# The weight splits behind three norms on VectorE, a third panel rounded before the second root, and the first two down panels interleaved by rows, in a two-layer decoder step

## The chip, the cores and the metric

The kernel runs on one core of one Trainium2 chip. A core has TensorE (matrix products into PSUM), VectorE, ScalarE, GpSimd (POOL in the profile), and SyncE, whose queue starts the loads. The metric is the device time of one execution in microseconds (us): lower is better.

## The reference

One inference step of a decoder with an S5 layer followed by a FoX attention layer, over 512 prompt tokens and 8 sample tokens. The width is 1024, so each activation is held as eight tiles of 128 channels by 520 tokens. What matters here is what stands around the norms and in the feed-forward part of both layers:

```python
x = x + rmsnorm(o, p['norm_mix_post'][l])
f, cp = conv_ffn(rmsnorm(x, p['norm_ffn_pre'][l]), p['w_up'][l], p['conv_w'][l],
                 p['conv_b'][l], p['w_down'][l], conv_prev[l])
x = x + rmsnorm(f, p['norm_ffn_post'][l])
...
def conv_ffn(h, w_up, cw, cb, w_down, prev):
    u = h @ w_up
    y, new_prev = causal_dwconv(u, prev, cw, cb)
    g, val = jnp.split(y, 2, axis=-1)
    return (jax.nn.silu(g) * val) @ w_down, new_prev
```

All of it is in float32, w_up is 1024 by 5632 and w_down is 2816 by 1024.

## The kernel before

**Products in three parts.** A float32 weight panel of 128 output channels is loaded into `raw[slot]` by SyncE, rounded by ScalarE into `w_hi[slot]` (`hi`, line 2062), and its rest `raw - w_hi` is written to `w_lo[slot]` by GpSimd (`lo`, line 919; a *split* below). TensorE adds w_hi·x_hi, w_hi·x_lo and w_lo·x_hi in PSUM (`product`, line 2546). There are two slots, taken in turn, so panel q+2 can be rounded only when panel q has been multiplied (`panel_done`), can be split only behind its rounding, and its PSUM banks must have been read (`panel_read`). Panels are numbered through the whole program. `PH[name]` holds a phase's rows per panel, panel count and first number.

**The phases.** `wout0`, `up00`, `down00`, `up01`, `down01` are the output projection and the feed-forward part of layer 0; `win1` is the input projection of layer 1; `wout1`, `up10`, `down10`, `up11`, `down11` follow for layer 1. The feed-forward width is done in two halves: an up phase has 22 panels of 8 rows of 128, in 11 pairs (gate and value), and a down phase 8 panels of 11 rows. A down panel's row k needs the k-th product of gate and value, `h_hi` and `h_lo`.

**Inside an up phase.** For each pair VectorE scales the PSUM result by `rstd` into `uc` (lines 1747 and 1748, which frees the banks), waits for ScalarE's first tap `yc` (line 2405), adds the two other taps (lines 1752 to 1758), does the same for the second panel, then multiplies by ScalarE's `sg = silu(...)` (line 2411) and writes `h_hi` and `h_lo` (lines 1763 to 1767). ScalarE's program for a pair is: round the even panel, `newconv`, `yc`, round the odd panel, `newconv`, `yc`, `silu`. [...] The pairs are a hardware loop (`act.Fori` in `run`); the compiler puts the loads of ScalarE's function tables (ACT_TABLE_LOAD) where a function needs another set, and at the head of a loop it must suit both the entry and the way back.

**At a norm.** `post_norm` on VectorE and `post` on ScalarE walk through 16 steps (two token halves by eight channel tiles): scale y, add to x, split x into `x_hi` (ScalarE) and `x_lo` (VectorE), and sum squares on TensorE for the next norm. TensorE starts on the first two panels behind the norm meanwhile (`first_pair`, line 2643). The constants `ROOT_1`, `HI_NEXT`, `ROOT_PRE` and `RECIP_PRE` say at which step ScalarE takes the root of the second half's statistics, rounds the second next panel, and takes the next norm's first root, and at which step VectorE inverts it. Before, GpSimd splits both panels and ScalarE rounds the third one (the first that TensorE multiplies behind `first_pair`) in the first turn of the phase's loop, behind the last root.

## Time and profile before

| | |
|---|---|
| time, median of 3 runs | 1584.65 us (1578.77 to 1586.68) |
| profiled execution | 1581.49 us, its span 1579.8 us, mean granted clock 0.951 |
| TensorE busy | 1431.8 us, 91% of the span |
| VectorE busy | 986.8 us, 62% |
| ScalarE busy | 625.3 us, 40% |
| GpSimd busy | 671.0 us, 42% |

Times in rows are microseconds from the span's start. In a row of the timeline the first number is the start, the second the length; a bracket gives how long the engine had been idle and who released it. A busy share is an average over all phases: what a change is worth in one phase is read there.

### The profile page before, as it was taken

Reading aid. Unit: us, or ns where it says so; the run is one execution under the profiler, and the core shown is the slowest. Engines: PE = TensorE matmul, PEld = TensorE weight load, DVE = VectorE, ACT = ScalarE, POOL = GpSimd, SP = SyncE. Lnnn points to the kernel's source line nnn. Section 1 sums busy time; section 2 is a strip of 40 time slices with the busy share of each in tenths; the row PEclk is TensorE's granted clock in tenths of the full one; section 3 lists DMA queues with packets and bytes.
Section 4 is the critical chain, followed back from the end, with each engine's and each line's share of the span. In section 5 each row is a group of like instructions: output and inputs, shape, how many; then the busy total and the mean of one; then the engine's idle time right before and its main releaser. Section 6 shows DMA issues by size and latency. Waiting matters only on the chain.

```text
span 1579.8 us, 32525 instructions
## 1 busy us (share of the span) xinstructions
PE 1431.8 (91%) x12097; PEld 1325.2 (84%) x12097; DVE 986.8 (62%) x1644; ACT 625.3 (40%) x1058; POOL 671.0 (42%) x429
## 2 busy tenths in 40 slices
PE   6987848988998999999898979998979999999997
PEld 6975637978998999999798966555969999999997
DVE  5769945577775056765847678642587772277755
ACT  4554533245663134332414225431356551234323
POOL 0686232313333444443277888401323443344440
PEclk9996978989999999999999999988989999999999
DMA  5444372222333223333044758995213233223321
GB/s 169 125 96 77 67 199 66 76 55 68 95 82 95 79 83 93 91 96 92 27 132 140 229 162 286 320 319 154 80 38 88 88 108 92 78 83 92 113 79 60
DMA packets 288905, 180.46 MB, mean 114 GB/s; under 512 B 54072, under 2 KB 274396, under 8 KB 288748
## 3 DMA queue, kind: packets, MB, share of 16 engines
q1 hardware_dynamic: 288812, 179.20, 39.3%
q8 instruction: 61, 1.00, 0.3%
q14 instruction: 32, 0.26, 0.1%
HBM read 167.10 MB, written 10.63 MB: 113 GB/s over the span
## 4 chain that ended last, share of the span: by engine, by line
PE 58%; issue 15%; DVE 12%; POOL 6%; ACT 3%; SPq 3%; DMA 2%; DVEq 1%; ACTq 0%; POOLq 0%
PE big L2546 48%; PE big L2612 3%; SPq L583 2%; PE misc L2697 2%; ACT yc L2405 1%; DVE y L1663 1%; POOL s5s L923 1%; POOL e_tmp L923 1%; DVE tmp L1202 1%; POOL e_r L923 1%; POOL e_i L923 1%; PE big L2643 1%; DVE rstd L1160 1%; DVE hf L1763 1%; DVE x_lo L1192 1%
## 5 line engine op out<-in xcount | busy, mean ns | idle before, releaser
L919 POOL TENSOR_TENSOR w_lo<-raw,w_hi 128x1024 fp32r<-128x1024 f32 (+2 forms) x163 | 427.3, 2622 | 741.1 <-ACT w_hi L2062 740.9
L2546 PE MATMUL big<-x_hi,w_hi 128*128 128x264 f32 x2008 | 414.8, 288 | 17.2 <-POOL w_lo L919 12.4
L2062 ACT ACTIVATE w_hi<-raw 128x1024 fp32r<-128x1024 f32 (+2 forms) x179 | 198.4, 1109 | 533.8 <-PE big L2546 494.3
L2546 PE MATMUL big<-x_hi,w_lo 128*128 128x264 f32 x2008 | 407.6, 285 | 0.0
L2546 PE MATMUL big<-x_lo,w_hi 128*128 128x264 f32 x2008 | 405.9, 284 | 0.0
L2546 PEld LDWEIGHTS big<-x_hi,w_hi 128*128 128x128 f32 x2008 | 312.0, 190 | 23.2 <-issue 16.3
L2546 PEld LDWEIGHTS big<-x_lo,w_hi 128*128 128x128 f32 x2008 | 311.8, 190 | 0.0
L2546 PEld LDWEIGHTS big<-x_hi,w_lo 128*128 128x128 f32 x2008 | 310.9, 190 | 0.0
L1752 DVE SCALAR_TENSOR_TENSOR yc<-uc,convw,yc 128x512 f32<-128x512 f32 x88 | 120.2, 1366 | 113.3 <-ACT yc L2405 113.3
L2546 PE MATMUL big<-h_hi,w_hi 128*128 128x264 f32 x616 | 126.1, 286 | 10.6 <-DVE h_lo L1767 9.2
L2546 PE MATMUL big<-h_lo,w_hi 128*128 128x264 f32 x616 | 124.9, 284 | 0.0
L2546 PE MATMUL big<-h_hi,w_lo 128*128 128x264 f32 x616 | 124.4, 283 | 0.0
L2546 PEld LDWEIGHTS big<-h_hi,w_hi 128*128 128x128 f32 x616 | 95.0, 190 | 11.8 <-DVE h_lo L1767 10.0
L2546 PEld LDWEIGHTS big<-h_hi,w_lo 128*128 128x128 f32 x616 | 95.3, 190 | 0.0
L2546 PEld LDWEIGHTS big<-h_lo,w_hi 128*128 128x128 f32 x616 | 95.2, 190 | 0.0
L1757 DVE SCALAR_TENSOR_TENSOR yc<-uc,convw,yc 128x512 f32<-128x512 f32 x88 | 84.7, 962 | 12.7 <-DVE yc L1755 0.2
L1056 POOL TENSOR_TENSOR areas<-areas,qb 128x768 f32<-128x768 f32 x41 | 75.1, 1847 | 11.8 <-DMA areas<-in_cache_k 10.8
L1780 DVE COPY y<-big 128x264 f32 (+1 forms) x32 | 12.2, 424 | 104.3 <-PE big L2546 104.3
L2405 ACT ACTIVATE yc<-uc,convw 128x520 f32<-128x520 f32 x88 | 72.3, 822 | 0.8
L1142 DVE TENSOR_TENSOR sumsq<-sumsq,sq 128x520 f32<-128x520 f32 x20 | 53.0, 2649 | 11.6 <-ACT sq L2361 9.9
L2401 ACT ACTIVATE newconv<-uc 128x10 f32 (+1 forms) x88 | 18.1, 205 | 103.9 <-DVE uc L1748 103.8
L2643 PE MATMUL big<-x_hi,w_hi 128*128 128x264 f32 (+1 forms) x96 | 38.2, 398 | 17.0 <-DVE x_lo L1192 16.6
(425 smaller groups left out, 2385.6 us busy)
## 6 DMA issues: line engine op xcount, KB each, us to landing
raw<-in_w_up SPq DMA_DIRECT2D x88, 512.0 KB, 3.9
raw<-in_w_down SPq DMA_DIRECT2D x32, 704.0 KB, 4.7
areas<-in_cache_v SPq DMA_DIRECT2D x42, 384.0 KB, 4.5
areas<-in_cache_k SPq DMA_DIRECT2D x41, 384.0 KB, 4.3
raw<-in_w_in SPq DMA_DIRECT2D x16, 512.0 KB, 4.2
raw<-in_w_out SPq DMA_DIRECT2D x16, 512.0 KB, 4.3
raw<-in_w_kv SPq DMA_DIRECT2D x12, 512.0 KB, 4.1
spare<-in_cache_k SPq DMA_DIRECT2D x12, 384.0 KB, 4.1
```

The costliest lines, as they stand in the source:

```text
L583: sp.dma_start(dst, src, **kw).then_inc(s_(sm), 16)
L919: pool.tensor_tensor(w_lo[slot][:, 0:kb, :], raw[slot][:, 0:kb, :], w_hi[slot][:, 0:kb, :].bitcast(F32), ALU.subtract).then_inc(lo_made, 1)
L923: own.do(pool.tensor_tensor(o, a_, b_, op))
L1056: own.tell(pool.tensor_tensor(p, p, qb[b % 2][:].rearrange("p (a d) -> p a d", a=2), ALU.mult), s_("k_product"), n + 1)
L1142: ins = V.tensor_tensor(sumsq[:], sumsq[:], sq[:, m % 2, :], ALU.add)
L1752: st(V.scalar_tensor_tensor(yy[:, 0:T], uu[:, 1:1 + T], w_[1], yy[:, 0:T], ALU.mult, ALU.add))
L1757: st(V.scalar_tensor_tensor(yy[:, 0:T], uu[:, 0:T], w_[0], yy[:, 0:T], ALU.mult, ALU.add))
L2062: A.activation(w_hi[slot][:, 0:kb, :], raw[slot][:, 0:kb, :], ACT.Copy).then_inc(hi_made, 1)
L2405: A.activation(yy[:], uu[:, 2:2 + NT], ACT.Identity, bias=convw[:, 1 - l, bass.ds(it + (f * KH + half * KF + 132), 1)], scale=convw[:, 1 - ...
L2546: ins = pe.matmul(big[2 * slot + b_][:, 0:c1 - c0], w[slot][:, k, :], r[:, c0:c1], start=(k == 0 and n_ == 0), stop=(k == kb - 1 and n_ == 2))
L2612: return pe.matmul(big[2 * slot + b_][:, 0:c1 - c0], w[slot][:, k, :], r[:, c0:c1], start=(k == 0 and n_ == 0), stop=(k == kb - 1 and n_ = ...
L2643: ins = pe.matmul(big[2 * slot + b_][:, 0:c1 - c0], w[slot][:, k, :], r[:, k, c0:c1], start=(k == 0 and n_ == 0), stop=(k == KD - 1 and n_ ...
```

## The change

Three things are changed. At the three norms that are followed by a projection (`wout0`, `down01`, `wout1`) VectorE splits the first two panels behind the norm, at steps 1 and 11 of `post_norm`, and GpSimd no longer does; `ROOT_1` goes from 4 to 6 and `HI_NEXT` from 5 to 8. ScalarE rounds the third panel before the last root, so `run` gets an argument `rounded=3` for `up00`, `up10` and `win1`: the first turn of its loop is then written out ahead of the loop, less that rounding. And in `down00` and `down10` TensorE multiplies rows 0 to 9 of both first panels, then row 10 of each, in `pair_by_rows`.

```diff
-ROOT_1, HI_NEXT, ROOT_PRE, RECIP_PRE = 4, 5, 10, 13
+ROOT_1, HI_NEXT, ROOT_PRE, RECIP_PRE = 6, 8, 10, 13
+LO_FIRST, LO_NEXT = 1, 11
...
                 if name == "win1":
-                    lo(base, base % 2, kb)
-                    lo(base + 1, (base + 1) % 2, kb)
                     for i in range(2, n):
...
                 first = 2 if name in ("glu", "up00", "up10") or n <= 2 else 0
-                for i in range(min(first, n) if name != "glu" else 0):
+                for i in range(n if n <= 2 else 0):
                     lo(base + i, (base + i) % 2, kb)
...
                         split_lo(k, x[:, k, c], gain(nxt, k, nl), c)
+                    if nxt is not None and i == LO_FIRST:
+                        lo(PH[ph][2] + 8)
+                    elif nxt is not None and i == LO_NEXT:
+                        lo(PH[ph][2] + 9)
...
-            def run(name, work=None, ahead=True, started=True):
+            def run(name, work=None, ahead=True, started=True, rounded=2):
...
                 pairs = n // 2
+                if rounded > 2:
+                    work(0, 0)
+                    hi(kb, base + 3)
+                    work(0, 1)
                 if pairs > 2:
-                    with act.Fori(0, pairs - 1) as it:
+                    with act.Fori(rounded - 2, pairs - 1) as it:
...
                         root_half(name, 0)
+                hi(KD, base + n + 2)
                 root_half(name, 1)
...
-                    run(f"up{l}{f}", work)
+                    run(f"up{l}{f}", work, rounded=2 if f else 3)
...
-                if isinstance(it, int) and half == 0:
+                if isinstance(it, int) and it and half == 0:
...
-            run("win1", first_queries)
+            run("win1", first_queries, rounded=3)
...
+            def pair_by_rows(base, rhs, wait_k):
+
+                for rows_ in (range(KH - 1), (KH - 1,)):
+                    for q in (base, base + 1):
+                        if rows_[0] == 0:
+                            pe.wait_ge(lo_made, q + 1)
+                            pe.wait_ge(panel_read, q - 1)
+                        for k in rows_:
+                            wait_k(k)
+                            xh, xl = rhs(k)
+                            for n_, (w, r) in enumerate(((w_hi, xh), (w_hi, xl), (w_lo, xh))):
+                                for b_, (c0, c1) in enumerate(HALF):
+                                    ins = pe.matmul(big[2 * (q % 2) + b_][:, 0:c1 - c0], w[q % 2][:, k, :], r[:, c0:c1],
+                                                    start=(k == 0 and n_ == 0), stop=(k == KH - 1 and n_ == 2))
+                        if rows_[0]:
+                            ins.then_inc(panel_done, 1)
...
                     if f == 0:
-                        phase(f"down{l}{f}", h_half, wait_k=h_made)
+                        pair_by_rows(PH[f"down{l}0"][2], h_half, h_made)
+                        phase(f"down{l}0", h_half, first=2)
                         continue
```

ScalarE's instructions of `up00` before, from the last root of the norm through the loop body (registers and branches left out). `sd` is the root, `w_hi` a rounding, `sg` the silu:

```order
L2091 ACTIVATE sd<-misc,eps 128x256
...
L2062 ACT_TABLE_LOAD
L2062 ACTIVATE w_hi<-raw 128x1024
...
L2405 ACTIVATE yc_122<-uc_120,convw 128x520
...
L2062 ACTIVATE w_hi<-raw 128x1024
...
L2405 ACTIVATE yc_123<-uc_121,convw 128x520
...
L2411 ACT_TABLE_LOAD
L2411 ACTIVATE sg<-yc_122 128x520
L2073 REGISTER_ALU
L2073 COMPARE_AND_BRANCH
```

The same place with the change: the first rounding stands ahead of the root, the rest of the first pair ahead of the loop, and the loop begins at the second rounding below.

```order
L2065 ACTIVATE w_hi<-raw 128x1024
L2098 ACTIVATE sd<-misc,eps 128x256
...
L2419 ACT_TABLE_LOAD
L2419 ACTIVATE sg<-yc_122 128x520
...
L2065 ACTIVATE w_hi<-raw 128x1024
...
L2413 ACTIVATE yc_122<-uc_120,convw 128x520
...
L2065 ACTIVATE w_hi<-raw 128x1024
...
L2413 ACTIVATE yc_123<-uc_121,convw 128x520
L2418 REGISTER_ALU
L2419 ACTIVATE sg<-yc_122 128x520
L2080 REGISTER_ALU
L2080 COMPARE_AND_BRANCH
```

Two table loads stood in the loop of `up00`; the written-out first pair now holds one, and the loop none. The same holds for `up10`.

TensorE at the first pair of `down00` before, around row 10 of the first panel (`big0` and `big1` are its banks, `big2` and `big3` the second panel's):

```order
L2546 MATMUL big0<-h_hi_118,w_lo0 128x264
L2546 MATMUL big1<-h_hi_118,w_lo0 128x256
L2546 MATMUL big0<-h_hi_118,w_hi0 128x264
L2546 MATMUL big1<-h_hi_118,w_hi0 128x256
L2546 MATMUL big0<-h_lo_119,w_hi0 128x264
L2546 MATMUL big1<-h_lo_119,w_hi0 128x256
```

And with the change, the last twelve matmuls of the two panels and what stands ahead of them:

```order
L2649 MATMUL big2<-h_hi_118,w_lo1 128x264
L2649 MATMUL big3<-h_hi_118,w_lo1 128x256
L2649 MATMUL big0<-h_hi_118,w_hi0 128x264
L2649 MATMUL big1<-h_hi_118,w_hi0 128x256
...
L2649 MATMUL big0<-h_hi_118,w_lo0 128x264
L2649 MATMUL big1<-h_hi_118,w_lo0 128x256
L2649 MATMUL big2<-h_hi_118,w_hi1 128x264
L2649 MATMUL big3<-h_hi_118,w_hi1 128x256
```

Row 10 of the first panel, the one that ends it, has moved behind rows 0 to 9 of the second, so both panels end within twelve matmuls.

## Rows read from the trace of the kernel before

**Rows 1.** Page, part 1: busy us, share of the span, instructions

```profile
PE 1431.8 (91%) x12097; PEld 1325.2 (84%) x12097; DVE 986.8 (62%) x1644; ACT 625.3 (40%) x1058; POOL 671.0 (42%) x429
```

**Rows 2.** Timeline of `up00`, one pair, engine by engine

```profile
470.68 1.28 ACT L2411 ACT_TABLE_LOAD   x1
...
472.63 1.28 ACT L2062 ACT_TABLE_LOAD   x1
473.93 1.06 ACT L2062 ACTIVATE w_hi<-raw 128x1024 fp32r<-128x1024 f32 x1
...
465.78 2.39 POOL L919 TENSOR_TENSOR w_lo<-raw,w_hi 128x1024 fp32r<-128x1024 f32 x1 [0.78 <-ACT w_hi L2062]
475.07 2.38 POOL L919 TENSOR_TENSOR w_lo<-raw,w_hi 128x1024 fp32r<-128x1024 f32 x1 [6.89 <-ACT w_hi L2062]
...
464.49 1.07 DVE L1752 SCALAR_TENSOR_TENSOR yc<-uc,convw,yc 128x512 f32<-128x512 f32 x1 [1.33 <-ACT yc L2405]
...
465.84 2.88 DVE L1757 SCALAR_TENSOR_TENSOR yc<-uc,convw,yc 128x512 f32<-128x512 f32 x1
...
471.85 0.75 DVE L1757 SCALAR_TENSOR_TENSOR yc<-uc,convw,yc 128x512 f32<-128x512 f32 x1
...
474.86 0.43 DVE L1747 TENSOR_TENSOR uc<-big,rstd 128x264 f32<-128x264 f32 x1
...
477.58 0.51 PE L2546 MATMUL big<-x_hi,w_hi 128*128 128x264 f32 x2 [0.65 <-POOL w_lo L919]
```

**Rows 3.** Timeline of `up00`, last turn (no table reload), and the `h_lo` before

```profile
486.29 3.22 POOL L919 TENSOR_TENSOR w_lo<-raw,w_hi 128x1408 fp32r<-128x1408 f32 x1 [5.80 <-ACT w_hi L2062]
...
474.24 0.70 DVE L1767 TENSOR_TENSOR h_lo<-hf,h_hi 128x520 f32 x1
...
486.56 3.52 DVE L1767 TENSOR_TENSOR h_lo<-hf,h_hi 128x520 f32 x1
490.00 0.42 DVE L1747 TENSOR_TENSOR uc<-big,rstd 128x264 f32<-128x264 f32 x1
```

**Rows 4.** Timeline, VectorE: first `uc` of `up00`; first, third, last pair of `up10`

```profile
363.24 0.43 DVE L1747 TENSOR_TENSOR uc<-big,rstd 128x264 f32<-128x264 f32 x1 [0.24 <-DVE uc L1726]
...
1179.30 0.43 DVE L1747 TENSOR_TENSOR uc<-big,rstd 128x264 f32<-128x264 f32 x1 [0.23 <-DVE uc L1726]
...
1202.82 0.43 DVE L1747 TENSOR_TENSOR uc<-big,rstd 128x264 f32<-128x264 f32 x1
...
1295.09 0.43 DVE L1747 TENSOR_TENSOR uc<-big,rstd 128x264 f32<-128x264 f32 x1
```

**Rows 5.** Windows, first pair of `up00` and `up10`: busy times, clock, DMA

```profile
363.00:375.70 12.70, 9.69 (x80) 9.70 (x81) 9.16 (x16) 7.52 (x10) 4.79 (x2) 1.00 0.31 86
1179.30:1191.80 12.50, 9.74 (x68) 9.74 (x69) 9.22 (x16) 7.35 (x10) 4.78 (x2) 0.86 0.29 86
```

**Rows 6.** Timeline of `up01`, whose loop holds no table load

```profile
578.43 1.06 ACT L2062 ACTIVATE w_hi<-raw 128x1024 fp32r<-128x1024 f32 x1 [3.34 <-PE big L2546]
```

**Rows 7.** Timeline of the first two panels of `down00` and of `down10`

```profile
502.70 0.80 PE L2546 MATMUL big<-h_hi,w_hi 128*128 128x264 f32 x2 [4.43 <-DVE h_lo L1767]
...
1307.95 0.51 PE L2546 MATMUL big<-h_hi,w_hi 128*128 128x264 f32 x2 [1.57 <-DVE h_lo L1767]
...
513.83 1.38 ACT L2062 ACTIVATE w_hi<-raw 128x1408 fp32r<-128x1408 f32 x1 [8.05 <-PE big L2546]
...
1316.86 1.38 ACT L2062 ACTIVATE w_hi<-raw 128x1408 fp32r<-128x1408 f32 x1 [6.50 <-PE big L2546]
```

**Rows 8.** Timeline of the norm between `wout0` and `up00`

```profile
329.97 3.10 DVE L1663 SCALAR_TENSOR_TENSOR y<-y,gains,rstd 128x264 f32<-128x264 f32 x2
...
341.79 0.49 DVE L1192 SCALAR_TENSOR_TENSOR x_lo<-x,gains,x_hi 128x264 fp32r<-128x264 f32 x1 [1.40 <-ACT x_hi L2103]
...
366.01 0.50 PE L2546 MATMUL big<-x_hi,w_hi 128*128 128x264 f32 x2 [3.37 <-POOL w_lo L919]
```

**Rows 9.** Tile `w_lo`, VectorE's splits in `win0`: ns min/median/max

```profile
L1149 DVE TENSOR_TENSOR w_lo<-raw,w_hi x16: 1207/1226/1705, 18.9 to 109.6; 128x1024 fp32r<-128x1024 f32 x16
```

## The prediction

> **What bounds the kernel now.** I read the busy shares first, then the waits of each phase that the change touches, then the timeline of single pairs of panels. TensorE is busy for 91% of the span and VectorE for 62% [rows 1], which looks like a kernel bound by its matmuls. The phases differ, though. Take the 10 pairs of `up10` that the rows span: from its third pair to its last, eight pairs take 1295.09 - 1202.82 = 92.27 us, 11.53 us each [rows 4]. There TensorE never waits; that is its own work. In `up00` nine pairs take 474.86 - 363.24 = 111.62 us, 12.40 us each [rows 2, 4], and TensorE stands 0.65 us for a split in the pair shown [rows 2]. What sets the 12.40 us is VectorE: it goes from one pair to the next with no wait but the ones for ScalarE's first tap `yc`, and its instructions stretch when GpSimd is in a split. Line 1757 takes 2.88 us around the split that starts at 465.78 [rows 2]; unhindered it takes 0.75 us (at 471.85), so 2.13 us are stall. Line 1752, at 1.07 us, loses another 0.32 us. The other split of the pair (475.07 to 477.45) falls mostly on the 1.3 us in which VectorE waits for `yc` anyway, and that is why it costs only those 0.32 us.
>
> So an up phase has two gaits. If TensorE is behind, ScalarE's roundings wait for it (3.34 us in `up01` [rows 6]), the splits fall where VectorE has time, and a pair takes 11.53 us. If VectorE is behind, roundings start as soon as ScalarE's program comes to them, and where the splits then fall decides the pair. The Trainium skill (SBUF — State Buffer, "SBUF: two separate sides") says that a VectorE operation with two SBUF inputs and a GpSimd operation take a shared port pair as an exclusive lock, and the loser blocks; by that rule, the trace agrees.
>
> **Part 1: the loads that vanish from the loop.** The order of ScalarE's instructions shows an effect that the edit does not name. With the first pair written out, the silu table is already loaded when the loop is entered, so both ACT_TABLE_LOADs leave the loops of `up00` and `up10`. They are 1.28 us each [rows 2]. ScalarE's order per pair is yc, load, silu, load, rounding. Without them the rounding at 473.93 starts 2.56 us earlier, at 471.4, and its split runs from about 472.5 to 474.9 instead of 475.07 to 477.45. TensorE does not hold it back: its panel has ended by then. But from line 1757 at 471.85 to the end of `h_lo` at 474.9 [rows 2, 3] VectorE works without a wait on operations that mostly read two SBUF tiles, and one of them has to stand out the split.
>
> What that costs can be read from the one turn that had no reload before: the last turn of `up00` [rows 3]. Its rounding follows the silu directly, the split runs from 486.29 for 3.22 us, and `h_lo` takes 3.52 us where it took 0.70 us a pair earlier: 2.82 us lost, 0.40 less than the split. That pair took 490.00 - 474.86 = 15.14 us. For a split of 2.38 us I take 2.38 - 0.40 = 2.0 us. The stall of line 1757 stays, since the odd rounding still follows yc at once. A pair then takes 12.40 - 0.32 + 2.0 = 14.1 us. TensorE, with 11.53 us of work, would stand 2.5 us in each.
>
> Does it get out of this gait? `up10` before did. Its first pair began like `up00`'s, but the clock was 0.86 there against 1.00 [rows 5], which held TensorE back by 12.5 x 0.14 = 1.75 us. At 12.40 us a pair TensorE has only 0.87 us to spare in each, so that was enough, ScalarE's odd rounding had to wait for TensorE, and from the third pair on the pair took 11.53 us. At 14.1 us TensorE has 2.6 us to spare in each pair, and one such dip is absorbed. So I expect the slow gait to hold through both phases.
>
> `up00`: nine pairs from 12.40 to 14.1, +15.3 us; the last pair keeps its 15.14 us. `up10`: ten pairs took 1295.09 - 1179.30 = 115.8 us [rows 4]; they will take 9 x 14.1 + 15.1 = 142.0 us, **+26.2 us**.
>
> Here a rule speaks against this. The Trainium skill (ScalarE: Activation LUTs, "What ACT_TABLE_LOAD costs") has a table switch at about 1.28 us for the load and 1.38 us more for a drain, and its advice is to have fewer of them. By that page alone 20 pairs with two loads less would be a gain; the sum above would have no +15.3 and no +26.2. The trace shows loads of 1.28 us with the next instruction right behind them. That ScalarE is relieved is true; it was not what VectorE waited for.
>
> **Part 2: down panels by rows.** Before, TensorE stands 4.43 us for the last `h_lo` in `down00` and 1.57 us in `down10` [rows 7]. Now it fills that time with rows 0 to 9 of the second panel. What is late next: both panels end together, and the third can be rounded only when the first has ended. Ten rows of six matmuls at 0.12 us are 7.2 us. In `down00` rows 0 to 9 of the first panel ended at 502.70 - 4.43 = 498.27; the second's would end at 505.5, the last rows at 506.2 and 506.9. Rounding 1.38 us [rows 7], split 3.22 us [rows 3] and hand-overs of 0.1 us bring the third panel to 510.9, a new wait of 4.0 us. Before it started when the second panel ended, at 513.8 [rows 7]. That is -2.9 us, measured from the last `uc` (490.00) 20.9 us instead of 23.8. In `down10` the same 20.9 us stand against 1316.86 - 1295.09 = 21.8 us [rows 4, 7]: -0.9 us. If `up10` were bound by TensorE, the new wait would cost more than it fills: 1306.38 + 7.2 + 0.7 + 4.7 = 1319.0 against 1316.9, +2.1 us.
>
> **Part 3: the norms.** GpSimd's split of the first panel stretched two of VectorE's scalings to 3.10 us, where an operation of that kind and shape takes 0.49 us: some 2.2 us lost [rows 8]. VectorE's own split takes 1.23 us [rows 9]. That is -1.0 us. The second split hinders one scaling for as long as they overlap, between 0 and 2 us, against another 1.23 us: I take nothing. With `ROOT_1` at 6 VectorE's wait of 1.40 us for `x_hi` [rows 8] goes, but the reciprocal two steps later needs that root: I take half, -0.7 us. The third rounding ahead of the root delays the root, the reciprocal and the first `uc` by up to 0.5 us: +0.4 us. Each norm gives -1.3 us. Bounds: +0.5 us if TensorE has to wait for the late split at step 11, -3.4 us if all of TensorE's wait behind the norm [rows 8] goes. The wait for the third panel's split does go, but behind it stands VectorE's `uc`, which frees the banks. Three norms: **-3.9 us**. `win1` gains only this.
>
> **The sum**, against the profiled execution's own 1581.5 us: +15.3 + 26.2 - 2.9 - 0.9 - 3.9 = +33.8, **1615 us**. The median of the runs shown is 3.2 us above that execution, and the three differ by 8 us; I say 1616. A measurement here tells about 0.5% (8 us) from no change.
>
> **The rivals.**
> - *Fast gait in both phases (1568 us).* Fewer table loads leave ScalarE free, TensorE binds `up00` and `up10` as it binds `up01`, whose loop has no load either [rows 6]. For it: `up01`. Against it: `up01` begins with TensorE behind VectorE, whereas behind a norm two panels are finished before the first `uc`, and VectorE would have to make good some 3 us while it loses 4. Price: from first `uc` to third down panel `up00` takes 513.8 - 363.2 = 150.6 us and `up10` 137.6; `up00` would fall to the latter, -13.0, by-rows costs 2.1 twice, norms -3.9: -12.7, and about 1 us more from `up10`'s first pairs. It decides if TensorE is held back by over 2.6 us in one pair. 0.16.
> - *One phase only (1592 us).* A dip of the clock tips one of the two: -3.9 + 15.3 - 2.9 + 2.1 = +10.6, or -3.9 - 13.0 + 2.1 + 26.2 - 0.9 = +10.5. 0.09.
> - *No effect in the loops (1576 us).* The even split costs VectorE no more than before: -3.9 - 2.9 + 2.1 = -4.7. Against it: the turn of rows 3. 0.07.
> - The forecast, slow gait in both: 0.68, with its own range 1603 to 1626 (2.2 us instead of 2.0 per split adds 4 us; norms at their bounds give -6 and +5; if the odd split's stall shrinks by 0.3 us, -6).
>
> **How the numbers follow.** Slower by over 0.5% (above 1592.6) holds the forecast and half of the one-phase case: 0.73. Faster (below 1576.7) holds the fast gait and a little of the no-effect case: 0.18. The rest is 0.09. The range that leaves out the fast gait and the ends of the forecast's is 1576 to 1626.
>
> **What the profile would show.** ACT_TABLE_LOAD once in each of `up00` and `up10`. From one `uc` of an even panel to the next, 14.1 us; two instructions among lines 1752 to 1767 of about 2.2 us more than usual in each pair; TensorE idle 2.5 us before even panels. In `down00` and `down10` no wait for `h_lo`, but some 4 us for the third panel's split. TensorE back behind the norms about 1.3 us earlier. Pairs of 11.5 us in `up00` would prove me wrong, and then the step that failed is that VectorE cannot catch up.

## The result, and the profile after

The changed kernel takes **1620.8 us** (median of 4 runs, 1617.9 to 1624.5) against 1581.7 us of the kernel before (4 runs, 1578.1 to 1586.7). The ratio is 1.0249, 95% interval 1.0218 to 1.0279: slower by 2.5%. The profiled execution took 1617.9 us, its span is 1616.2 us, 36.4 us longer than before (1579.8).

Page of the changed kernel, part 1 (it answers to [rows 1]):

```profile
PE 1448.9 (90%) x12097; PEld 1340.6 (83%) x12097; DVE 1027.1 (64%) x1650; ACT 571.8 (35%) x1020; POOL 655.7 (41%) x423
```

ScalarE lost 53.5 us of work, GpSimd 15.3 us. VectorE has six instructions more, and is busy 40.3 us longer: six splits of 1.22 us are 7.3 of them. The rest is no work, but instructions that got longer.

Timeline of the changed kernel, the second pair of `up00`: ScalarE, GpSimd, VectorE, TensorE (start, duration, engine, line, operation; in brackets the idle time before it and who ended it). It answers to [rows 2].

```profile
375.18 0.82 ACT L2413 ACTIVATE yc<-uc,convw 128x520 f32<-128x520 f32 x1
375.91 1.04 ACT L2065 ACTIVATE w_hi<-raw 128x1024 fp32r<-128x1024 f32 x1
...
381.82 0.62 ACT L2419 ACTIVATE sg<-yc 128x520 f32<-128x520 f32 x1
382.35 1.04 ACT L2065 ACTIVATE w_hi<-raw 128x1024 fp32r<-128x1024 f32 x1
...
377.03 2.40 POOL L920 TENSOR_TENSOR w_lo<-raw,w_hi 128x1024 fp32r<-128x1024 f32 x1 [4.01 <-ACT w_hi L2065]
383.47 2.64 POOL L920 TENSOR_TENSOR w_lo<-raw,w_hi 128x1024 fp32r<-128x1024 f32 x1 [4.05 <-ACT w_hi L2065]
...
374.04 0.43 DVE L1750 TENSOR_TENSOR uc<-big,rstd 128x264 f32<-128x264 f32 x1
...
377.18 2.79 DVE L1760 SCALAR_TENSOR_TENSOR yc<-uc,convw,yc 128x512 f32<-128x512 f32 x1
...
383.10 0.75 DVE L1760 SCALAR_TENSOR_TENSOR yc<-uc,convw,yc 128x512 f32<-128x512 f32 x1
383.76 2.37 DVE L1761 SCALAR_TENSOR_TENSOR yc<-convs,convw,yc 128x8 f32<-128x8 f32 x1
...
388.25 0.43 DVE L1750 TENSOR_TENSOR uc<-big,rstd 128x264 f32<-128x264 f32 x1
...
374.85 0.51 PE L2554 MATMUL big<-x_hi,w_hi 128*128 128x264 f32 x2 [2.06 <-DVE uc L1751]
```

The reader is to see three things. No load stands between `sg` and the second rounding. Both of GpSimd's splits now begin just as VectorE is about to start an operation that reads two SBUF tiles. And each holds one up: line 1760 takes 2.79 us where its twin takes 0.75, line 1761, an operation on eight columns, takes 2.37 us where it takes 0.22. That is 2.04 and 2.15 us of stall, 4.19 in a pair. The pair takes 388.25 - 374.04 = 14.21 us (14.15 on the mean of the nine from 360.17, whose first is shorter), and TensorE stands 2.06 us in it.

The span by stages, from VectorE's `uc` and reciprocals in the two traces. A down stage runs from the last pair's first `uc` to the first `uc` of the next up phase.

| stage | before | after | difference | predicted |
|---|---|---|---|---|
| up to the first norm's reciprocal | 327.79 | 326.35 | -1.4 | 0 |
| norm 1, reciprocal to first `uc` | 35.45 | 33.82 | -1.6 | -1.3 |
| `up00`, first to last pair | 126.8 | 142.2 | +15.4 | +15.3 |
| `down00` | 76.9 | 78.1 | +1.2 | -2.9 |
| norm 2, first to last reciprocal | 32.25 | 31.82 | -0.4 | -1.3 |
| attention, to the third norm | 357.8 | 352.9 | -4.9 | 0 |
| norm 3, reciprocal to first `uc` | 35.8 | 35.2 | -0.6 | -1.3 |
| `up10`, first to last pair | 115.8 | 142.4 | +26.6 | +26.2 |
| `down10` | 74.8 | 76.9 | +2.1 | -0.9 |

These add up to the 36.4 us; the stages left out differ by under 0.1 us. The attention stage begins with `win1`, whose first pair is written out by the edit, but up to the `y` that VectorE makes of its seventh panel it took 35.4 us in both traces; behind it nothing is changed. The stage took between 351.3 and 357.8 us in the 14 traces of this study, and 356.3 and 353.0 us in two traces of one and the same kernel, so I take -4.9 as that scatter and no effect.

The down phases lost where I had forecast a gain. Timeline of the changed kernel, TensorE's waits in `down00` and at its like in `down10` (they answer to [rows 7]), then windows of `down00` (from:to, length, busy times with counts of TensorE, its weight loads, VectorE, ScalarE and GpSimd, then the granted clock, DMA share, GB/s):

```profile
503.23 0.77 PE L2649 MATMUL big<-h_hi,w_hi 128*128 128x264 f32 x2 [2.92 <-issue]
524.74 0.79 PE L2554 MATMUL big<-h_hi,w_hi 128*128 128x264 f32 x2 [4.06 <-POOL w_lo L920]
...
1350.38 0.80 PE L2554 MATMUL big<-h_hi,w_hi 128*128 128x264 f32 x2 [4.06 <-POOL w_lo L920]
```

```profile
520.00:522.00 2.00, 0.68 (x6) 0.47 (x4) 1.50 (x4) 2.00 (x2) 0.55 (x1) 1.00 0.00 0
522.00:524.00 2.00, 0.00 (x0) 0.00 (x0) 0.00 (x0) 0.64 (x1) 2.00 (x1) 0.84 0.00 0
524.00:526.00 2.00, 1.26 (x6) 1.27 (x7) 0.00 (x0) 0.00 (x0) 2.00 (x2) 0.50 0.06 16
526.00:528.00 2.00, 2.00 (x11) 2.00 (x11) 0.00 (x0) 0.00 (x0) 1.74 (x1) 0.50 0.96 278
528.00:530.00 2.00, 2.00 (x11) 2.00 (x11) 0.00 (x0) 0.00 (x0) 0.00 (x0) 0.50 0.38 75
530.00:532.00 2.00, 2.00 (x18) 2.00 (x17) 0.00 (x0) 0.00 (x0) 0.00 (x0) 0.96 0.52 142
```

The wait for `h_lo` is gone; for the 2.92 us ahead of the first panel the profile names nobody. The wait for the third panel's split is there as forecast, 4.06 us. Behind it the granted clock stands at 0.50 for 6 us, and TensorE does 11 matmuls in 2 us instead of 18. The prediction had the wait and not the clock behind it.

Last, TensorE at the first norm of the changed kernel:

```profile
346.78 0.39 PE L2668 MATMUL big<-x_hi,w_hi 128*128 128x264 f32 x1 [2.37 <-DVE w_lo L1148]
```

VectorE's second split, at step 11, comes 2.37 us too late for TensorE.

### The profile page after: what moved, and what is told of

It is laid out like the page before. It is cut to its first block, busy times and chain, and to the rows that moved or that the text cites. A ratio compares the mean times of both kernels' runs of the same rounds, so it can differ in the third digit from the quotient of the medians.

```text
span 1616.2 us, 32465 instructions
## 1 busy us (share of the span) xinstructions
PE 1448.9 (90%) x12097; PEld 1340.6 (83%) x12097; DVE 1027.1 (64%) x1650; ACT 571.8 (35%) x1020; POOL 655.7 (41%) x423
## 4 chain that ended last, share of the span: by engine, by line
PE 46%; issue 34%; DVE 8%; POOL 7%; DMA 2%; ACT 1%; SPq 1%; POOLq 0%; DVEq 0%; ACTq 0%
PE big L2554 37%; POOL w_lo L920 6%; PE misc L2722 2%; PE big L2620 2%; DVE tmp L1201 1%; SPq L584 1%; PE big L2920 1%; DVE bp L1201 1%; PE misc L3120 1%; DVE sc L1852 1%; DVE y L1662 1%; DMA yz<-y_scratch 1%; DVE cp L1201 1%; PE big L3150 1%; DVE x_lo L1191 0%
## 5 line engine op out<-in xcount | busy, mean ns | idle before, releaser
L920 POOL TENSOR_TENSOR w_lo<-raw,w_hi 128x1024 fp32r<-128x1024 f32 (+2 forms) x157 | 412.5, 2628 | 796.6 <-ACT w_hi L2065 796.4
L2554 PE MATMUL big<-x_hi,w_hi 128*128 128x264 f32 x2008 | 420.3, 291 | 37.9 <-DVE uc L1751 33.8
L2554 PE MATMUL big<-h_hi,w_hi 128*128 128x264 f32 (+1 forms) x528 | 109.5, 289 | 11.3 <-POOL w_lo L920 8.1
L2554 PE MATMUL big<-h_lo,w_hi 128*128 128x264 f32 (+1 forms) x528 | 108.0, 286 | 0.0
L2554 PE MATMUL big<-h_hi,w_lo 128*128 128x264 f32 (+1 forms) x528 | 107.8, 286 | 0.0
L2554 PEld LDWEIGHTS big<-h_hi,w_hi 128*128 128x128 f32 x528 | 82.7, 193 | 12.3 <-issue 8.5
L2554 PEld LDWEIGHTS big<-h_lo,w_hi 128*128 128x128 f32 x528 | 82.8, 193 | 0.0
L2554 PEld LDWEIGHTS big<-h_hi,w_lo 128*128 128x128 f32 x528 | 82.7, 193 | 0.0
L1141 DVE TENSOR_TENSOR sumsq<-sumsq,sq 128x520 f32<-128x520 f32 x20 | 53.2, 2661 | 11.7 <-ACT sq L2368 10.0
L1761 DVE SCALAR_TENSOR_TENSOR yc<-convs,convw,yc 128x8 f32<-128x8 f32 x88 | 59.6, 678 | 0.0
```

The source lines that it names most:

```text
L920: pool.tensor_tensor(w_lo[slot][:, 0:kb, :], raw[slot][:, 0:kb, :], w_hi[slot][:, 0:kb, :].bitcast(F32), ALU.subtract).then_inc(lo_made, 1)
L1141: ins = V.tensor_tensor(sumsq[:], sumsq[:], sq[:, m % 2, :], ALU.add)
L1761: V.scalar_tensor_tensor(yy[:, T:NT], old[:, 0], w_[0], yy[:, T:NT], ALU.mult, ALU.add).then_inc(s_("conv_made"), 1)
L2554: ins = pe.matmul(big[2 * slot + b_][:, 0:c1 - c0], w[slot][:, k, :], r[:, c0:c1], start=(k == 0 and n_ == 0), stop=(k == kb - 1 and n_ == 2))
```

## The experiments

Twelve runs were made, of eleven kernels (no_rows_again is waits_no_rows once more). Lengths of pairs are worked out from the starts of line "uc, 128x264" in the profiled execution, the steady pair as the mean of the third to the ninth; ratios are to the kernel before, with a 95% interval.

| run | median us | ratio (interval) | `up00` / `up10`, first to last pair | steady pair |
|---|---|---|---|---|
| before | 1581.7 | | 126.8 / 115.8 | 12.40 / 11.53 |
| after | 1620.8 | 1.0249 (1.0218 to 1.0279) | 142.2 / 142.4 | 14.18 |
| round3 | 1620.4 | 1.0271 (1.0248 to 1.0295) | 142.4 / 142.4 | 14.18 |
| rows | 1578.2 | 0.9978 (0.9953 to 1.0004) | 126.8 / 115.8 | 12.40 / 11.53 |
| vsplits | 1563.9 | 0.9905 (0.9889 to 0.9922) | 116.9 / 115.6 | 11.53 |
| vsplits_rows | 1572.8 | 0.9960 (0.9931 to 0.9989) | 115.8 / 116.8 | 11.53 |
| reload | 1611.1 | 1.0204 (1.0182 to 1.0225) | 135.3 / 135.2 | 13.9 |
| reload_once | 1576.1 | 0.9983 (0.9954 to 1.0013) | 117.1 / 117.2 | 11.53 |
| waits | 1567.7 | 0.9939 (0.9907 to 0.9970) | 112.6 / 112.6 | 11.53 |
| waits_no_rows | 1559.5 | 0.9886 (0.9797 to 0.9976) | 112.6 / 112.6 | 11.53 |
| before_waits | 1575.0 | 0.9972 (0.9946 to 0.9998) | 119.4 / 120.0 | 11.75 / 11.83 |
| half_splits (work left out) | 1580.6 | 1.0008 (0.9985 to 1.0031) | 121.3 / 121.6 | 11.98 |
| no_rows_again | 1560.7 | 0.9889 (0.9853 to 0.9925) | 112.6 / 112.6 | 11.53 |
| splits_earlier | 1554.9 | 0.9851 (0.9816 to 0.9887) | 112.6 / 112.6 | 11.53 |

### The three parts alone

**round3.** Of the change only the third panel's rounding and the written-out first pair:

```diff
+                if rounded > 2:
+                    work(0, 0)
+                    hi(kb, base + 3)
+                    work(0, 1)
...
+                hi(KD, base + n + 2)
                 root_half(name, 1)
```

> The kernel of before with one part of the change alone: the third panel is rounded ahead of the root and the first pair is written out; GpSimd makes all splits of before, the down panels go as before. By my theory this part alone takes the loads out of the loops and holds the whole loss: pairs of 14.1 us in up00 and up10, 15 and 26 us more, about 1622 us (1618 to 1628). If the longer pairs needed VectorE's splits at the norms or the down panels by rows to come about, the kernel stays at 1577 to 1587 us with pairs of 12.4 and 11.5 us.

Measured: 1620.4 us, pairs of 14.18 us. This part alone holds the whole loss. VectorE's splits and the down panels have no hand in the long pairs.

**rows.** Only `pair_by_rows` and its call:

```diff
-                        phase(f"down{l}{f}", h_half, wait_k=h_made)
+                        pair_by_rows(PH[f"down{l}0"][2], h_half, h_made)
+                        phase(f"down{l}0", h_half, first=2)
```

> The kernel of before with the first down panels by rows alone. My prediction gave this part -3.8 us in all. The changed kernel's trace showed less: the third down panel began 1.5 and 0.8 us earlier, but TensorE's clock stood at half level for some 6 us behind the new wait of 4.06 us, and the stretch from there was 2.7 and 2.9 us longer. By that, this part costs about 2 us in down10 and 1 to 2 in down00: 1582 to 1587 us in all. By the prediction's own terms, 1576 to 1580 us. The pairs of the up phases stay at 12.4 and 11.5 us by either.

Measured: 1578.2 us, inside what no measurement here tells from no change; neither side is borne out by the sum. The two phases differ. From the last panel's `uc` to the next phase's first, `down00` took 69.4 us (70.2 before), `down10` 74.3 us (70.0 before). In front of `down10` TensorE had only 1.57 us to fill [rows 7], and got this instead (run rows, TensorE's wait and two windows behind it):

```profile
1313.02 0.50 PE L2546 MATMUL big<-h_hi,w_hi 128*128 128x264 f32 x2 [4.06 <-POOL w_lo L919]
```

```profile
1309.00:1313.00 4.00, 0.00 (x0) 0.00 (x0) 0.89 (x3) 1.92 (x2) 3.27 (x2) 1.00 0.00 0
1313.00:1317.00 4.00, 3.98 (x22) 3.98 (x23) 0.00 (x0) 0.00 (x0) 3.04 (x1) 0.63 0.62 177
```

4.06 us of wait for 1.57, and 22 matmuls in a window that otherwise holds 36. In `down00` the kernel before already had such a stretch, behind its wait of 4.43 us, and in `down10`, behind 1.57 us, it had none. Windows of the kernel before, `down00` twice and `down10`:

```profile
502.00:504.00 2.00, 1.30 (x6) 1.30 (x7) 0.64 (x1) 0.00 (x0) 0.00 (x0) 0.50 0.04 3
504.00:506.00 2.00, 2.00 (x11) 2.00 (x11) 0.76 (x2) 1.38 (x1) 0.14 (x1) 0.50 0.02 4
...
1308.00:1310.00 2.00, 2.00 (x17) 2.00 (x18) 0.76 (x2) 1.02 (x1) 0.00 (x0) 1.00 0.02 5
```

So the panels by rows exchange one low stretch for another in `down00`, and add one in `down10`.

**vsplits.** Only VectorE's splits at the norms, with the new step numbers:

```diff
-ROOT_1, HI_NEXT, ROOT_PRE, RECIP_PRE = 4, 5, 10, 13
+ROOT_1, HI_NEXT, ROOT_PRE, RECIP_PRE = 6, 8, 10, 13
+LO_FIRST, LO_NEXT = 1, 11
...
+                    if nxt is not None and i == LO_FIRST:
+                        lo(PH[ph][2] + 8)
+                    elif nxt is not None and i == LO_NEXT:
+                        lo(PH[ph][2] + 9)
```

> The kernel of before with VectorE's splits at the norms alone (the first of the next panels' splits as step 1, the second as step 11), and the places of the first root, the rounding ahead and so on moved with them. Predicted for the norms: -1.3 us at each of three, -3.9 in all: about 1577.5 us. The changed kernel showed -1.6, -0.4 and -0.6 there, and TensorE waiting 2.4 us for the second split at each: by that -2.6 us, about 1579 us. The pairs should be 12.4 and 11.5 us; if the gait hangs on where the loop is entered, they may be of either length, which this run would show: 14.1 us a pair would bring 15 us or more.

Measured: 1563.9 us, 1% faster. Far more than the norms give: `up00` went to 11.53 us a pair from its third pair on, 9.9 us in all. Its loop holds two loads a turn, as before, and the same instructions: the same code has two rhythms. What differs at its start is the clock. Behind the wait for the third panel's split, 3.37 us here as in [rows 8], the granted clock fell to 0.50, where before it stayed at 1.00. Window of the first pair of `up00` in run vsplits, to be held against the first row of [rows 5]:

```profile
362.63:375.11 12.48, 9.71 (x59) 9.71 (x60) 9.18 (x16) 7.32 (x10) 4.78 (x2) 0.73 0.31 86
```

59 matmuls instead of 80: TensorE is held back by 12.48 x 0.27 = 3.4 us, far more than the 0.87 us a pair that it has to spare at 12.40. That is what the prediction gave as the reason why `up10` was fast before. The traces of before, rows, vsplits and vsplits_rows hold eight up phases with this loop. In two, `up00` of before and of rows, the first pair had a clock of 1.00, and the pairs settled at 12.40 us; in the other six it had 0.86 or 0.73, and they settled at 11.53. No run changes the clock alone, so this is a match in eight of eight and not an isolated cause, and why the clock fell behind one wait of 3.37 us and not behind another is not shown.

Run vsplits, the pair of `up00` from 410.32, GpSimd and VectorE:

```profile
409.83 2.84 POOL L920 TENSOR_TENSOR w_lo<-raw,w_hi 128x1024 fp32r<-128x1024 f32 x1 [3.35 <-ACT w_hi L2065]
415.60 2.42 POOL L920 TENSOR_TENSOR w_lo<-raw,w_hi 128x1024 fp32r<-128x1024 f32 x1 [2.93 <-ACT w_hi L2065]
...
410.32 0.43 DVE L1750 TENSOR_TENSOR uc<-big,rstd 128x264 f32<-128x264 f32 x1
...
412.41 0.80 DVE L1755 SCALAR_TENSOR_TENSOR yc<-uc,convw,yc 128x512 f32<-128x512 f32 x1 [1.33 <-ACT yc L2408]
...
416.50 2.06 DVE L1755 SCALAR_TENSOR_TENSOR yc<-uc,convw,yc 128x512 f32<-128x512 f32 x1 [1.28 <-ACT yc L2408]
```

The first split lies over `uc`, which reads PSUM banks, and over VectorE's 1.33 us of waiting; the other over 0.9 us of waiting and then line 1755. Stall: 0.05 and 1.31 us, where the changed kernel has 4.19.

**vsplits_rows.** Both of these edits.

> The kernel of before with VectorE's splits at the norms and the down panels by rows, without the third panel's rounding ahead. The run vsplits alone took 1563.9 us, since its up00 ran at 11.5 us a pair, not 12.4. If the by-rows part costs 2 to 3 us here as its clock dips say, 1565 to 1568 us; if it saves what rows alone seemed to, 1559 to 1563 us. If up00 falls back to 12.4 us a pair, because where the loop is entered decides, 1574 to 1580 us.

Measured: 1572.8 us, 8.9 us slower than vsplits, though `up00` and `up10` keep their 11.53 us. From the last panel's `uc` to the next phase it takes 73.9 us in `down00` and 74.1 in `down10`; vsplits takes 70.3 in both. That is 7.4 of the 8.9 us. Behind a fast loop, the panels by rows cost some 4 us each.

### The loads

**reload.** After, with a one-column square root behind the even silu in the loops:

```diff
                             A.activation(sg[:], yc[0][:], ACT.Silu).then_inc(s_("silu_made"), 1)
+                            if not isinstance(it, int) and f == 0:
+                                A.activation(root_warm[:], eps[:], ACT.Sqrt)
```

> The changed kernel with one tiny square root of ScalarE behind each even panel's silu in the loops of up00 and up10: nothing of the work changes, but the table loads come back into the loops (one for the square root, one for the rounding, one for the silu), 1.28 us each by [rows 2]. My theory, that the pair is 14.15 us long because the rounding of the even panel comes without a load in front of it and so GpSimd's split of that panel starts while VectorE converts: the split is moved 2.6 us later, mostly into VectorE's wait, the pairs go back to 11.5 to 12.5 us, and the kernel takes 1578 to 1592 us. The rival, that the third panel's rounding and the first pair written out set the rhythm by where the loop is entered, whatever loads it holds: pairs stay at 14.15 us and the kernel at 1621 us or above.

Measured: 1611.1 us, pairs of 13.9 us. Neither side of my forecast came true, and the edit wasn't clean: the loop now held three loads a turn, for the silu, for the square root and for the even panel's rounding, so that this rounding came 1.5 us later behind the silu than in the kernel before; the odd one has no load ahead of it. Run reload, two splits and the two additions they meet:

```profile
430.14 2.39 POOL L920 TENSOR_TENSOR w_lo<-raw,w_hi 128x1024 fp32r<-128x1024 f32 x1 [8.78 <-ACT w_hi L2065]
433.19 2.40 POOL L920 TENSOR_TENSOR w_lo<-raw,w_hi 128x1024 fp32r<-128x1024 f32 x1 [0.66 <-ACT w_hi L2065]
...
431.02 2.06 DVE L1755 SCALAR_TENSOR_TENSOR yc<-uc,convw,yc 128x512 f32<-128x512 f32 x1 [1.83 <-ACT yc L2413]
...
433.36 2.77 DVE L1760 SCALAR_TENSOR_TENSOR yc<-uc,convw,yc 128x512 f32<-128x512 f32 x1
```

The delayed split moved from line 1761 to line 1755 of the next pair, and with the other it still costs 1.31 + 2.02 us. More loads alone do not help; the place of the splits does.

**reload_once.** So the square root goes outside the loop, once, which restores the two loads of before in each turn:

```diff
                     work(0, 1)
+                    if name != "win1":
+                        A.activation(root_warm[:], eps[:], ACT.Sqrt)
```

> The changed kernel with one tiny square root of ScalarE behind the written-out first pair of each even-numbered up phase, outside the loop. The loop then has exactly the two table loads of before in each turn (one ahead of the even panel's rounding, one ahead of the silu) and not the three that the run reload had, where both roundings were moved and the pairs took 13.9 us. My theory (the pair's length is set by where in the pair the two roundings fall, and so where GpSimd's splits lie): pairs of 12.40 or of 11.53 us, both of which loops with two loads have shown, so 1582 to 1598 us or 1565 to 1580 us. The rival (the loads themselves matter little; the third panel's rounding ahead of the root and the late end of the loop do): 14.1 us a pair and 1618 to 1624 us.

Measured: 1576.1 us. One square root of 0.20 us more than in the changed kernel, with the loads that it brings back, and it is 44.7 us faster. After three pairs of 11.7, 13.9 and 10.9 us in `up00` the loop runs at 11.53. The missing loads are the cause of the long pairs. That the loop settled at 11.53 and not at 12.40 goes with the clock again: it was 0.88 in the second pair of both phases. In the changed kernel, where TensorE has 2.6 us to spare in a pair, 0.88 or 0.89 stood in three pairs of `up00` and four of `up10`, and all its pairs stayed long.

### The place of the splits

**half_splits.** After, with GpSimd computing half of each `w_lo` in the two loops (work left out):

```diff
-                            lo(it * 2 + (base + first + half), (base + half) % 2, kb)
+                            lo(it * 2 + (base + first + half), (base + half) % 2, kb // 2 if name in ("up00", "up10") else kb)
```

> The changed kernel, in which GpSimd computes only the first half of w_lo (four of eight rows of blocks) for the panels of its loops in up00 and up10: work is left out, so the time can't be compared as a whole. Nothing else is touched, and ScalarE's roundings stand where they stood. In the changed kernel VectorE's two additions that a split falls on took 2.79 and 2.37 us instead of 0.75, and a free split takes 2.35 us. My theory, that the added 2.6 us over the fast pair are VectorE held up while GpSimd splits: with splits of some 1.2 us the additions take at most 1.6 us each, and the pairs are 11.5 to 12.2 us long. The rival, that the splits slow nothing but only coincide, and the pair is set by the roundings or by TensorE: 14.1 us as before this edit.

Measured, pairs of 11.98 us; GpSimd and the two additions of one pair and the pair before it:

```profile
428.49 1.51 POOL L920 TENSOR_TENSOR w_lo<-raw,w_hi 128x512 fp32r<-128x512 f32 x1 [4.05 <-ACT w_hi L2065]
435.13 1.29 POOL L920 TENSOR_TENSOR w_lo<-raw,w_hi 128x512 fp32r<-128x512 f32 x1 [5.13 <-ACT w_hi L2065]
...
428.78 1.25 DVE L1761 SCALAR_TENSOR_TENSOR yc<-convs,convw,yc 128x8 f32<-128x8 f32 x1
...
435.29 1.69 DVE L1760 SCALAR_TENSOR_TENSOR yc<-uc,convw,yc 128x512 f32<-128x512 f32 x1
```

The stalls are 1.03 and 0.94 us, 2.22 less than the 4.19 of the changed kernel's pair of 14.21 us; the pair is 2.23 us shorter. Take the stalls away and three kernels give the same number for VectorE's own pair: 14.21 - 4.19 = 10.02, 11.98 - 1.97 = 10.01, and before, where the pair of [rows 2] took 12.46 us, 12.46 - 2.13 - 0.32 = 10.01 us. So VectorE bounds these loops, by its work plus the time it is held up.

**waits.** After, with two waits of ScalarE, `beside`, ahead of the two roundings of a pair in the up phases (`dve_at` is VectorE's count at the phase's start, ten to a pair):

```diff
+                    def beside(it, half):
+                        if half:
+                            act.wait_ge(dve_step, it * 10 + (dve_at[l, f] + 2))
+                        elif not isinstance(it, int) or it:
+                            act.wait_ge(dve_step, it * 10 + (dve_at[l, f] - 1))
```

> The changed kernel, with no load put back, but with two waits of ScalarE: the rounding ahead of each odd panel waits until VectorE has made the first of its two additions for the even panel, and the rounding ahead of the even one until VectorE has made hf of the pair before, so that both of GpSimd's splits begin at a chosen place of VectorE's order. My theory: the splits then lie mostly in VectorE's waits for yc and beside its short operations, whatever the loads do, and the pairs of up00 and up10 are 11.5 us long (13.9 or less at the worst): 1562 to 1575 us. The rival, that the missing loads lengthen the pair in another way than by the place of the splits (or that TensorE has become its bound): 14.1 us a pair and 1618 us or above.

Measured: 1567.7 us, 53 us below the changed kernel, pairs of 11.53 us in both phases without a single load in the loops. Run waits, the pair of `up00` from 432.09, ScalarE's roundings, GpSimd and VectorE:

```profile
430.98 1.07 ACT L2068 ACTIVATE w_hi<-raw 128x1024 fp32r<-128x1024 f32 x1 [3.87 <-DVE hf L1769]
436.22 1.06 ACT L2068 ACTIVATE w_hi<-raw 128x1024 fp32r<-128x1024 f32 x1 [2.20 <-PE big L2567]
...
432.12 2.40 POOL L920 TENSOR_TENSOR w_lo<-raw,w_hi 128x1024 fp32r<-128x1024 f32 x1 [3.88 <-ACT w_hi L2068]
437.36 2.42 POOL L920 TENSOR_TENSOR w_lo<-raw,w_hi 128x1024 fp32r<-128x1024 f32 x1 [2.83 <-ACT w_hi L2068]
...
434.17 0.91 DVE L1758 SCALAR_TENSOR_TENSOR yc<-uc,convw,yc 128x512 f32<-128x512 f32 x1 [1.32 <-ACT yc L2426]
438.26 2.06 DVE L1758 SCALAR_TENSOR_TENSOR yc<-uc,convw,yc 128x512 f32<-128x512 f32 x1 [1.28 <-ACT yc L2426]
```

The even rounding stands 3.87 us at its new wait, and the splits hold VectorE up by 0.16 and 1.31 us instead of 4.19. A third way to the fast pair, by nothing but later roundings, and without a dip of the clock: it was 1.00 in all twenty pairs.

**waits_no_rows.** The same without `pair_by_rows`.

> The kernel of the run waits, but with the first down panels in the order of before. By the trace of the changed kernel the panels by rows brought 1.5 and 0.8 us and cost 2.7 and 2.9 us at half clock, so this kernel should be 3 us faster than waits. The run rows alone said otherwise: 0.2% faster than before, interval from 0.5% faster to none; by that this kernel is 0 to 4 us slower than waits.

Measured: 1559.5 us, 8.2 us faster than waits, more than either side said. The two down stages take 69.8 and 70.1 us instead of 74.1 and 74.8: 9.0 us.

**before_waits.** The two waits alone in the kernel before.

> The kernel of before with nothing but the two waits of ScalarE in the up phases, which the run waits put into the changed kernel. There they gave pairs of 11.5 us in both phases. My theory: the same here, so up00 falls from 12.40 to 11.5 us a pair, 8 to 11 us in all, and up10 stays: 1568 to 1574 us. If the roundings, with a table load in front of the even one, come too late behind these waits, the pairs are 12 to 13 us long in both and nothing is won: 1580 to 1595 us.

Measured: 1575.0 us. `up00` gained 7.3 us, `up10` lost 4.2: pairs of 11.75 and 11.83 us. With loads in the loop, the even rounding starts 1.3 us behind its wait (1.28 us of load), and the waits alone are not enough for TensorE's 11.53. By this trace the loads are in the way here; no run tries it alone.

**splits_earlier and no_rows_again.** waits_no_rows with the second split two steps earlier, and the same kernel unchanged beside it:

```diff
-ROOT_1, HI_NEXT, ROOT_PRE, RECIP_PRE = 6, 8, 10, 13
-LO_FIRST, LO_NEXT = 1, 11
+ROOT_1, HI_NEXT, ROOT_PRE, RECIP_PRE = 6, 7, 10, 13
+LO_FIRST, LO_NEXT = 1, 9
```

> The kernel of the run waits_no_rows with VectorE's second split at each norm as step 9 instead of 11, and the rounding ahead of it as step 7 instead of 8. TensorE waited 2.37 us for that split at each of the three norms. If that wait is on the path to the next reciprocal, 1.0 to 2.4 us are won at each, 3 to 7 us in all, against the run beside it; if the reciprocal waits for VectorE's own order, as the waits of 1.2 us before split and addition would say, nothing: within 1.5 us.

> The kernel of the run waits_no_rows once more, beside the run splits_earlier and with more rounds: 1557 to 1562 us, 1.3% below before.

Measured: 1554.9 us (1551.4 to 1556.5) against 1560.7 us (1558.1 to 1564.2), no overlap. Run splits_earlier, TensorE at the first norm:

```profile
345.64 0.39 PE L2664 MATMUL big<-x_hi,w_hi 128*128 128x264 f32 x1 [0.45 <-DVE w_lo L1150]
```

0.45 us instead of 2.37. From the first to the last reciprocal of the norms it takes 31.3, 31.4 and 31.3 us, no_rows_again 31.7, 33.6 and 33.2: 4.5 us of the 5.9. The wait was on the path, but most of its price is the clock behind it. Run after, windows behind the same wait of 2.37 us at the first and at the third norm:

```profile
346.78:348.78 2.00, 2.00 (x14) 1.93 (x15) 1.81 (x5) 0.46 (x2) 0.00 (x0) 1.00 0.25 69
...
1172.26:1174.26 2.00, 2.00 (x9) 1.90 (x9) 1.80 (x5) 0.00 (x0) 0.00 (x0) 0.50 0.25 69
```

Nine traces have the second split at step 11, so 27 norms. In 11 the clock stayed at 1.00 behind the wait, and first to last reciprocal took 31.7 to 32.0 us; in 16 it was down to 0.50 there, and it took 33.0 to 34.5. The wait alone is worth the 0.4 us between 31.7 and 31.3; with the low clock behind it, some 2 us. This kernel is the best of all, 1.5% below the one before and 4.1% below the changed one.

## Why the prediction was right, and where not

**Part 1, the loads: right, by its mechanism and its sizes.** 14.15 us a pair for 14.1, +15.4 and +26.6 us for +15.3 and +26.2. That the missing loads do it is shown by reload_once, that they do it through the splits' place by waits and half_splits. The stall that I put at 2.0 us for the even split measured 2.15, and the odd one stayed at 2.04. It fell on line 1761, and not on `h_lo` as in [rows 3]. TensorE stands 2.06 us a pair, for 2.5 forecast. That the slow pair would hold through a dip of the clock was right too: `up10` kept its long pairs from start to end, though four of them had a clock of 0.88 or 0.89.

**The rule on SBUF's ports.** Line 1761, with two SBUF inputs, waited out a split, and so did a conversion with one input, in the changed kernel's first pair:

```profile
370.62 2.40 POOL L920 TENSOR_TENSOR w_lo<-raw,w_hi 128x1024 fp32r<-128x1024 f32 x1 [5.29 <-ACT w_hi L2065]
...
370.66 2.64 DVE L1768 CAST h_hi<-hf 128x520 f32 x1
```

It takes 0.43 us when free. `uc`, from PSUM, took 0.43 us inside a split (run vsplits, 410.32). The Trainium skill (SBUF — State Buffer, "SBUF: two separate sides") names as those that take the pair VectorE's operations with two SBUF inputs and those in a two-port mode; the trace agrees for both kinds if the conversion ran in such a mode, which no row here tells.

**The loads' own price.** Before, the instruction behind a load started 0.02 us after its end [rows 2]. The Trainium skill (ScalarE: Activation LUTs, "What ACT_TABLE_LOAD costs") adds a drain of 1.38 us to each switch; the trace does not agree, since from the load's start at 472.63 to the rounding at 473.93 it is 1.30 us in all. The Trainium skill's rule to batch activation calls by table set (ScalarE: Activation LUTs, "Table sets: the hidden batching unit"), which makes for fewer loads, would here have had the wrong sign.

**Part 2, the down panels: the step that failed is -2.9 and -0.9 us.** They measured +1.2 and +2.1. The new wait of 4.0 us was right (4.06). Two things were not in the sum. The first panel began in a stretch of low clock, so the third began 22.4 us behind the last `uc` and not 20.9; and behind the 4.06 us the clock stood at half: from the third panel to the next norm's reciprocal it took 242.4 us, 239.7 before. In `down10` the third panel came as forecast (-0.8 us), and only the clock behind it (+2.9 us) was missing. In seven stages behind 11.53 us pairs the by-rows order took 73.9 to 74.8 us (once in rows, twice each in vsplits_rows, waits and reload_once) against 69.8 to 70.3 without it. It gains nothing reliable even behind slow pairs (69.4 in rows for 70.2 before; 71.5 in the changed kernel for 69.8 in round3). The rival's bound of +2.1 us for a fast `up10` was half of the truth.

**Part 3, the norms: -3.9 forecast, -2.6 measured in the changed kernel.** The first split's -1.0 is a gain: in run vsplits the two scalings took 0.89 us and not 3.10. The second split was costed at nothing; it holds up TensorE by 2.37 us at each norm, and splits_earlier got back 4.5 us in three norms. This was named as the bound of +0.5 us a norm, and should have been a term. How much of the -2.6 is the edit's can't be told from these two traces: in the second half of the norm, the clock fell to 0.50 at the first and third norm of the kernel before, and at the third alone of the changed one.

**The sum.** 33.8 us forecast, 36.4 measured: +0.5 on the loops, +7.1 on the down panels, +1.3 on the norms, and -6.3 in front of the first norm and in the attention stage, where no edit shows. The near hit owes something to that scatter: without it the loss is 42.7 us, which by 1581.5 us is 1624 us, close to the upper end of the range.

**The rival of a fast gait** was the more instructive half. It was right that both phases can run at 11.53 us; the edit simply did not lead there, while VectorE's splits alone did for `up00`, which I had not forecast at all. The prediction's own account of `up10`, a clock below 1.00 in the first pair, fits all eight phases with the loop of before; that the clock would fall in `up00` of vsplits was beyond it. The kernel before itself took 1564 to 1569 us in 4 of its 65 runs and 1577 to 1587 in 57; that these few had `up00` in the fast rhythm fits the 10 us, but none of them has a trace.

## What to carry to other kernels

In a loop where GpSimd and VectorE both work on SBUF, what counts is when a GpSimd instruction starts against VectorE's order: taking 2.6 us off a third engine can cost 2 us a turn. Look up what releases it, and pin that to a place in VectorE's order by a wait rather than leave it to the lengths of instructions; such a loop can otherwise have several steady rhythms, and what happens in its first pairs, here a dip of TensorE's clock, goes with which one it keeps. And where filling an idle stretch of TensorE makes two results come at once, count the wait that follows them, and the clock behind it.

## What the runs showed that I had not expected

- One loop, unchanged, has at least two stable rhythms (12.40 and 11.53 us a pair, before and vsplits), the faster one wherever the clock was below 1.00 in the first pair; with three loads a turn or none it has others (13.9 and 14.18).
- The clock behind a wait of 4.06 us was granted at 0.50 for 6 us in the changed kernel's `down00`, but averaged 0.63 over the 4 us behind the same wait in `down10` of run rows. Behind the same wait of 2.37 us at a norm it stayed at 1.00 or fell to 0.50. What makes the difference was not tried.
- A VectorE operation on eight columns (0.22 us) that meets a split of 2.64 us is held for 2.15 us, and one on 512 columns for 2.04: the price goes with GpSimd's instruction and not with VectorE's.
